# The scan's period in a hybrid decoder layer: twelve halves of weights a block in place of sixteen

## The chip, the cores and the metric

The kernel runs on one core of one Trainium2 chip. Its time is the device time of an execution in microseconds; several runs are taken and their median is given. The profile shows one execution. Five engines run their own programs and meet through semaphores: TensorE (PE, matmuls into the accumulation memory PSUM), VectorE (DVE), ScalarE (ACT), GpSimd (POOL, here only for transfers) and SyncE (SP, transfers).

## The reference

One layer of a decoder trunk on 576 tokens (512 of a prompt, 64 of eight samples with a state of their own). In essence:

```python
proj = x @ w_in                              # 2048 x 10240: u, z_a, b, c, h, z_c, g_a, g_c
# A) state space: 64 groups of 16 channels, a complex diagonal state of 64 per group
bu = einsum(u_group, bb)                     # input matrix, from lam and b
h  = associative_scan(lam, bu) + lam**t * h0
y  = Re(c @ h) + d * u
y  = gelu(y); y = y * sigmoid(y @ w_glu)
y_a = (y * silu(z_a)) @ w_out_a
# B) gated convolution of width 3
y_c = (b * conv3(c * h_c)) * silu(z_c) @ w_out_c
out = (sigmoid(g_a) * y_a + sigmoid(g_c) * y_c) @ w_o
x   = layernorm(alpha * x + out)             # also returned: the last states and convolution rows
```

All values are float32.

## The kernel before, in words

All weights stream through the core in *halves*: one half is 128 output features by 1024 input features. SyncE loads a half into one of three buffers `w_raw`. ScalarE copies it, rounded, to `w_hi` (its `split`, L764), VectorE writes the rest to `w_lo` (its `split`, L979), and TensorE multiplies: 48 matmuls of 288 columns per half for the three products hi·hi, hi·lo, lo·hi (`half`, L634). Halves are numbered h. The stretches are: u (h = 0 to 15), the convolution (16 to 79, eight halves per group of channels, l = (h − 16) mod 8), z_a (80 to 95), the gates g (96 to 159), then w_glu, w_out_c, w_out_a and w_o.

Each engine has a loop over h. In the step of h ScalarE and VectorE first split half h + 2, then do what the stretch wants (evacuate PSUM, gate, convolve), then `scan_steps(h)`. ScalarE's split of h + 2 waits until TensorE has ended half h − 1, since the buffer is used again. What reads a half's result waits for `half_done` of h + 1, which means the end of half h: in the convolution ScalarE at l = 1 and 7, VectorE at l = 3, 5 and 7; in z_a both at odd h; in the gates ScalarE at odd h.

The scan of the state space (A) runs beside this, from h = 16 on, in eight blocks of eight groups. `ssm_step(h, off)` gives the block b whose step `off` falls on half h: block b starts at S = 16 + SSM_PER·b, and its steps count halves from there. A block goes so (before, with the step in brackets):

- GpSimd loads the block's matrices (`load_mats`, −1) and u (`load_u`, 2).
- VectorE makes the table of rotations (`turn_table`, 0), the input matrix (1) and the output matrix with the small taps (2).
- ScalarE rounds the output matrix to `lch` (4), the input matrix to `lbh` and u to `uh` (5). VectorE writes the rests: `lcl` (5), `lbl` and `ul` (6).
- TensorE makes the input products (`states_in`, L656, L657) and the taps (`taps`) ahead of half S + 7. They wait for `lbl` and `ul`.
- ScalarE evacuates (7), VectorE adds (8, 9), GpSimd swaps the halves of partitions (`v_sw`, 9), VectorE runs the scan proper (`scan`, 11), GpSimd swaps again (12) and stores the taps (11) and loads them shifted, as `lth` and `ltl`, by 16 transfers (`load_lt`, 13). VectorE turns back (`turn_back`, 14); its result `st` lies in `u_raw`'s place.
- ScalarE rounds the states to `hh` (15), VectorE writes the rest `hl` (17).
- TensorE makes the outputs (`outputs`, L679 to L682) ahead of half S + 19. They wait for `hl`, `lcl` and the taps, and each engine takes its instructions in order, so the half behind waits too.
- ScalarE, VectorE: GELU (19 to 23). GpSimd stores y (`store_y`, 25).

GpSimd runs without splits. Its loop over h only sets the order of its transfers; each waits for its semaphore.

Of the kernel before, what the change touches and what calls it, by code (L numbers as in the profile page):

```python
# [60 lines left out]
SSM0 = H_CONV  # L61
SSM_PER = 16
Y_LOAD = SSM0 + SSM_PER * (BLK - 1) + 23

# [30 lines left out]
def build(nc, d):  # L95
# [79 lines left out]
    out_st = [r(f"out_st{i}", [P, TOK]) for i in range(4)]  # L175
    st = u_raw
    uh, ul = (u2[:, :, i, :] for i in range(2))
# [353 lines left out]
    def _(pool):  # L531
# [21 lines left out]
        def load_u(b):  # L553
            for s in range(2):
                pool.wait_ge(u_stored[s], 16 * (b + 2 - s) // 2 if b < NB - 1 else 16 * NB // 2)
            if b:
                pool.wait_ge(hl_ready, b)
            src = u_dram[b].rearrange("(g c) (j k) -> j c g k", c=GC, k=CH)
            for j in range(T):
                pool.dma_start(u_raw[GC * j:GC * j + GC, :, :], src[j]).then_inc(u_loaded, 16)  # L560
# [27 lines left out]
        def scan_moves(h):  # L588
            if (b := ssm_step(h, -1)) is not None:
                load_mats(b)  # L590
            if (b := ssm_step(h, 2)) is not None:
                load_u(b)
            if (b := ssm_step(h, 9)) is not None:
                pool.wait_ge(v_ready, b + 1)
                swap(v_sw, v_st, v_swapped)
            if (b := ssm_step(h, 12)) is not None:
                pool.wait_ge(s_ready, b + 1)
                swap(v_sw, v_st, s_swapped)
            if (b := ssm_step(h, 11)) is not None:
                store_k(b)  # L600
            if (b := ssm_step(h, 13)) is not None:
                load_lt(b)
            if (b := ssm_step(h, 25)) is not None:
                store_y(b)

        store_mq()
        for h in range(SSM0 - 1, SSM0 + SSM_PER * (BLK - 1) + 26):
            scan_moves(h)

    @blk.tensor  # L610
    def _(pe):
# [83 lines left out]
        for h in range(H_CONV, H_GLU):  # L695
            if (b := ssm_step(h, 7)) is not None:
                states_in(b)
                taps(b)
            if (b := ssm_step(h, 19)) is not None:
                outputs(b)  # L700
            par = (h // 2) % 2
            if h % 2 == 0:
                fresh(par)
            half(h, par, xh, xl, h % 2 * KH, h % 2 == 0, h % 2 == 1)
# [51 lines left out]
    def _(act):  # L756
# [23 lines left out]
        def scan_steps(h):  # L780
            if (b := ssm_step(h, 19)) is not None:
                act.wait_ge(y_done, b + 1)
                if b:
                    act.wait_ge(y_stored, U_LOAD * b)
                for y, o in zip(in_banks(y_pre), of_scan(0)):
                    act.activation(y, o, ACT.Copy).then_inc(y_evac, 1)
            if (b := ssm_step(h, 4)) is not None:
                act.wait_ge(lc_ready, b + 1)
                if b:
                    act.wait_ge(y_done, b)  # L790
                act.activation(lch[:, :, :, :].rearrange("p g t c -> p g (t c)"),
                               lc[:, :, 1:, :].rearrange("p g t c -> p g (t c)"), ACT.Copy).then_inc(lch_ready, 1)
            if (b := ssm_step(h, 5)) is not None:
                act.wait_ge(lb_ready, b + 1)
                act.activation(lbh[:, :, :], mb[:, :, :, :].rearrange("p g c s -> p g (c s)"), ACT.Copy)\
                   .then_inc(lbh_ready, 1)
                act.wait_ge(u_loaded, U_LOAD * (b + 1))
                act.activation(uh, u_raw[:, :, :], ACT.Copy).then_inc(uh_ready, 1)
            if (b := ssm_step(h, 7)) is not None:
                act.wait_ge(v_done, b + 1)  # L800
                if b:
                    act.wait_ge(st_ready, b)
                for v, o in zip(in_banks(v_st), of_scan(0)):
                    act.activation(v, o, ACT.Copy).then_inc(v_evac, 1)
            if (b := ssm_step(h, 7)) is not None:
                act.wait_ge(k_done, b + 1)
                if b:
                    act.wait_ge(kl_ready, b)
                act.activation(k_st[:, :, :].rearrange("p h n -> p (h n)"), k_ps[:, 0:2 * P], ACT.Copy)\
                   .then_inc(k_evac, 1)  # L810
            if (b := ssm_step(h, 10)) is not None:
                act.wait_ge(kd_ready, b + 1)
                if b:
                    act.wait_ge(k_stored, 32 * b)
                act.activation(k_hi[:, :, :], k_st[:, :, :], ACT.Copy).then_inc(kh_ready, 1)
            if (b := ssm_step(h, 15)) is not None:
                act.wait_ge(st_ready, b + 1)
                act.activation(last_state[:, b * NG:(b + 1) * NG, :], st[:, :, CP - 1:], ACT.Copy)
                act.activation(hh[:, :, 1:CP], st[:, :, 0:CP - 1], ACT.Copy)
                act.activation(hh[:, :, CP:], h0[:, 0, b * NG:(b + 1) * NG, :], ACT.Copy).then_inc(hh_ready, 1)  # L820
            if (b := ssm_step(h, 22)) is not None:
                act.wait_ge(y_arg, b + 1)
                act.activation(scr[0][:, 0:COLS], scr[0][:, 0:COLS], ACT.Sigmoid, scale=GELU_S).then_inc(y_sig, 1)
# [144 lines left out]
    def _(dve):  # L968
# [190 lines left out]
        def turn_table(b):  # L1159
            gs = slice(b * NG, (b + 1) * NG)  # L1160
            f = [fine[:, 0:T, c, gs].rearrange("p r g -> p g r").unsqueeze(2).to_broadcast([P, NG, T, T])
                 for c in (0, 1)]
            k, ks = ([t[:, 0:T, c, gs].rearrange("p a g -> p g a").unsqueeze(3).to_broadcast([P, NG, T, T])
                      for c in (0, 1)] for t in (coarse, coarse_s))
            s = [x[:, 0:NG * CP].rearrange("p (g a r) -> p g a r", g=NG, r=T) for x in scr]
            for out, a, op in ((cos, (k[0], k[1]), ALU.subtract), (sins, (ks[1], ks[0]), ALU.add)):
                own.mark(dve.tensor_tensor(s[0], a[0], f[0], ALU.mult))
                link(dve.tensor_tensor(s[1], a[1], f[1], ALU.mult))
                link(dve.tensor_tensor(grid(out), s[0], s[1], op))
# [39 lines left out]
        def scan(b):  # L1209
            s = [x[:, 0:COLS] for x in scr]  # L1210
            dve.wait_ge(v_swapped, 32 * (b + 1))
            own.mark(dve.tensor_tensor(s[0], flat(v_st), flat(cos), ALU.mult))
            link(dve.tensor_tensor(s[1], flat(v_sw), flat(sins), ALU.mult))
# [6 lines left out]
        def turn_back(b):  # L1220
            s = [x[:, 0:COLS] for x in scr]
            dve.wait_ge(s_swapped, 32 * (b + 1))
            own.mark(dve.tensor_tensor(s[0], flat(v_st), flat(cos), ALU.mult))
            link(dve.tensor_tensor(s[1], flat(v_sw), flat(sins), ALU.mult))
            dve.wait_ge(ul_ready, b + 1)
            dve.tensor_tensor(flat(st), s[0], s[1], ALU.subtract).then_inc(st_ready, 1)

        def scan_steps(h):
            if (b := ssm_step(h, 17)) is not None:
                dve.wait_ge(hh_ready, b + 1)  # L1230
                own.mark(dve.tensor_tensor(hl[:, :, 1:CP], st[:, :, 0:CP - 1], hh[:, :, 1:CP].bitcast(F32), ALU.subtract))
                dve.tensor_tensor(hl[:, :, CP:], h0[:, 0, b * NG:(b + 1) * NG, :], hh[:, :, CP:].bitcast(F32),
                                  ALU.subtract).then_inc(hl_ready, 1)
            if (b := ssm_step(h, 0)) is not None:
                turn_table(b)
            if (b := ssm_step(h, 1)) is not None:
                input_matrix(b)
            if (b := ssm_step(h, 2)) is not None:
                output_matrix(b)
            if (b := ssm_step(h, 8)) is not None:  # L1240
# [4 lines left out]
                dve.sem_inc(v_sum, 1)  # L1245
            if (b := ssm_step(h, 20)) is not None:
                dve.wait_ge(y_evac, 2 * b + 2)
# [3 lines left out]
                dve.sem_inc(y_sum, 1)  # L1251
            if (b := ssm_step(h, 5)) is not None:
                dve.wait_ge(lch_ready, b + 1)
# [4 lines left out]
            if (b := ssm_step(h, 6)) is not None:  # L1258
# [4 lines left out]
                dve.tensor_tensor(ul, u_raw[:, :, :], uh.bitcast(F32), ALU.subtract).then_inc(ul_ready, 1)  # L1263
            if (b := ssm_step(h, 9)) is not None:
                chunk_sums(b)
            if (b := ssm_step(h, 11)) is not None:
                dve.wait_ge(kh_ready, b + 1)
                dve.tensor_tensor(k_lo[:, :, :], k_st[:, :, :], k_hi[:, :, :].bitcast(F32), ALU.subtract)\
                   .then_inc(kl_ready, 1)
            if (b := ssm_step(h, 11)) is not None:  # L1270
                scan(b)
            if (b := ssm_step(h, 14)) is not None:
                turn_back(b)
            if (b := ssm_step(h, 21)) is not None:
                dve.wait_ge(y_sum, b + 1)
# [3 lines left out]
                dve.scalar_tensor_tensor(s, s, 1.0, y, ALU.add, ALU.mult).then_inc(y_arg, 1)  # L1279
            if (b := ssm_step(h, 23)) is not None:  # L1280
                dve.wait_ge(y_sig, b + 1)
# [330 lines left out]
```

## Time and profile before

| | |
|---|---|
| median of 3 runs | 1577.32 us (1576.9 to 1578.0) |
| the profiled execution | 1577.16 us, span 1575.3 us |
| TensorE busy | 1545.9 us, 98% of the span |
| VectorE busy | 830.0 us, 53% |
| ScalarE busy | 444.3 us, 28% |
| GpSimd busy | 189.0 us, 12% |
| granted clock of TensorE, mean | 0.995 of full |
| traffic of memory | 136 GB/s over the span |

A busy share is a mean over the whole span. TensorE's rows are matmuls that overlap: a matmul of 288 columns lasts some 296 ns in the profile while the next starts some 133 ns later (6.40 us for 48), so a row's end lies behind the next row's start. In a timeline the bracket at the end of a row gives the time for which the engine was idle ahead of it and what ended that.

### The profile page before, as it was taken

Reading aid. Unit: us, or ns where it says so; the run is one execution under the profiler, and the core shown is the slowest. Engines: PE = TensorE matmul, PEld = TensorE weight load, DVE = VectorE, ACT = ScalarE, POOL = GpSimd, SP = SyncE. Lnnn points to the kernel's source line nnn. Section 1 sums busy time; section 2 is a strip of 40 time slices with the busy share of each in tenths; the row PEclk is TensorE's granted clock in tenths of the full one; section 3 lists DMA queues with packets and bytes.
Section 4 is the critical chain, followed back from the end, with each engine's and each line's share of the span. In section 5 each row is a group of like instructions: output and inputs, shape, how many; then the busy total and the mean of one; then the engine's idle time right before and its main releaser. Section 6 shows DMA issues by size and latency. Waiting matters only on the chain.

```text
span 1575.3 us, 26995 instructions
## 1 busy us (share of the span) xinstructions
PE 1545.9 (98%) x11690; PEld 1539.2 (98%) x11690; DVE 830.0 (53%) x1177; ACT 444.3 (28%) x582; POOL 189.0 (12%) x348
## 2 busy tenths in 40 slices
PE   8999999999999999999999999999999999999994
PEld 8999999999999999999999999999999999999994
DVE  5977374464463553643633533223733355666887
ACT  4222222222122122222222222133411122333444
POOL 0110040230311311302204113010000000000000
PEclk9999999999999999999999999999999999999997
DMA  9352362452543543634625535344544443555573
GB/s 304 125 152 91 92 166 79 116 158 75 133 133 94 146 117 122 176 109 132 161 83 165 136 115 147 104 156 150 189 141 134 125 127 125 160 187 183 183 221 107
DMA packets 87447, 221.21 MB, mean 140 GB/s; under 512 B 19744, under 2 KB 28576, under 8 KB 87328
## 3 DMA queue, kind: packets, MB, share of 16 engines
q1 hardware_dynamic: 71456, 188.78, 38.6%
q0 software_dynamic: 15872, 30.70, 8.6%
q8 instruction: 92, 1.51, 0.4%
q14 instruction: 27, 0.22, 0.0%
HBM read 186.55 MB, written 28.16 MB: 136 GB/s over the span
## 4 chain that ended last, share of the span: by engine, by line
PE 94%; DVE 3%; SPq 1%; DMA 1%; issue 1%; ACT 0%; DVEq 0%
PE acc L634 91%; SPq L420 1%; DMA w_raw<-in_w 1%; PE s_ps L656 1%; DVE r_all L1495 0%; PE s_ps L680 0%; PE s_ps L682 0%; DVE w_lo L979 0%; DVE r_all L1494 0%; PE s_ps L657 0%; PE s_ps L681 0%; PE s_ps L679 0%; PE k_ps L666 0%; DVE rstd L1488 0%; DVE r_all L1460 0%
## 5 line engine op out<-in xcount | busy, mean ns | idle before, releaser
L634 PE MATMUL acc<-xh,w_hi 128*128 128x288 f32 x2560 | 550.9, 297 | 3.9 <-DVE xl L987 3.7
L634 PE MATMUL acc<-xh,w_lo 128*128 128x288 f32 x2560 | 549.5, 296 | 0.0
L634 PE MATMUL acc<-xl,w_hi 128*128 128x288 f32 x2560 | 549.2, 296 | 0.0
L979 DVE TENSOR_TENSOR w_lo<-w_raw,w_hi 128x1024 fp32r<-128x1024 f32 x263 | 321.8, 1224 | 406.8 <-ACT w_hi L764 405.1
L764 ACT ACTIVATE w_hi<-w_raw 128x1024 fp32r<-128x1024 f32 x263 | 278.0, 1058 | 597.3 <-PE acc L634 578.2
L634 PEld LDWEIGHTS acc<-xh,w_hi 128*128 128x128 f32 x2560 | 412.9, 189 | 6.4 <-DVE w_lo L997 2.3
L634 PEld LDWEIGHTS acc<-xh,w_lo 128*128 128x128 f32 x2560 | 413.4, 188 | 0.0
L634 PEld LDWEIGHTS acc<-xl,w_hi 128*128 128x128 f32 x2560 | 413.4, 188 | 0.0
L634 PE MATMUL acc<-mh,w_hi 128*128 128x288 f32 x512 | 152.2, 297 | 1.0 <-DVEq L983 0.7
L634 PE MATMUL acc<-ml,w_hi 128*128 128x288 f32 x512 | 151.3, 296 | 0.0
L634 PE MATMUL acc<-mh,w_lo 128*128 128x288 f32 x512 | 151.3, 296 | 0.0
L634 PEld LDWEIGHTS acc<-mh,w_hi 128*128 128x128 f32 x512 | 96.1, 188 | 1.7 <-DVEq L983 0.9
L634 PEld LDWEIGHTS acc<-ml,w_hi 128*128 128x128 f32 x512 | 96.1, 188 | 0.2
L634 PEld LDWEIGHTS acc<-mh,w_lo 128*128 128x128 f32 x512 | 96.1, 188 | 0.0
L887 ACT ACTIVATE out_st<-acc 128x576 f32<-128x576 f32 x32 | 20.9, 654 | 189.6 <-PE acc L634 189.6
L564 POOL DMA_DIRECT2D v_sw<-v_st x32 | 18.3, 577 | 446.4 <-DVE v_st L1204 417.7
L634 PE MATMUL acc<-gcl,w_hi 128*128 128x288 f32 x256 | 55.0, 296 | 0.0
L634 PE MATMUL acc<-gch,w_lo 128*128 128x288 f32 x256 | 55.0, 296 | 0.0
L634 PE MATMUL acc<-gal,w_hi 128*128 128x288 f32 x256 | 55.0, 296 | 0.0
L634 PE MATMUL acc<-gah,w_hi 128*128 128x288 f32 x256 | 55.0, 296 | 0.0
L634 PE MATMUL acc<-gah,w_lo 128*128 128x288 f32 x256 | 54.9, 296 | 0.0
L634 PE MATMUL acc<-gch,w_hi 128*128 128x288 f32 x256 | 54.9, 296 | 0.0
(275 smaller groups left out, 1467.1 us busy)
## 6 DMA issues: line engine op xcount, KB each, us to landing
w_raw<-in_w SPq DMA_DIRECT2D x263, 512.0 KB, 3.8
sg_dram<-out_st SPq DMA_DIRECT2D x32, 288.0 KB, 4.6
v_sw<-v_st POOLq DMA_DIRECT2D x32, 144.0 KB, 3.9
gc_in<-sg_dram SPq DMA_DIRECT2D x16, 288.0 KB, 2.7
sz_in<-sg_dram SPq DMA_DIRECT2D x16, 288.0 KB, 2.7
x_in<-in_xT SPq DMA_DIRECT2D x32, 144.0 KB, 2.2
outT<-o_st SPq DMA_DIRECT2D x32, 144.0 KB, 1.8
mb<-mq_dram POOLq DMA_DIRECT2D x8, 512.0 KB, 6.6
```

Of the source, the lines that this page charges most:

```text
L420: sp.dma_start(k_dram[part, b, :, :, 0:KROW - T * GC].rearrange("x p n -> p x n"), zeros[:, :, :]).then_inc(zeros_stored, 16)
L564: pool.dma_start(to[64 * x:64 * x + 64, :, :], of[64 - 64 * x:128 - 64 * x, :, :]).then_inc(done, 16)
L634: ins = pe.matmul(acc[:, par, t, 0:TH], w, m[:, k0 + k, t * TH:(t + 1) * TH], start=first and k == 0 and n == 0, stop=last and k == KH - 1 ...
L656: pe.matmul(out_of(g), lbh[:, g, :], u, start=True, stop=False)
L764: act.activation(w_hi[h % NW][:, :], w_raw[:, h % NW, :], ACT.Copy).then_inc(hi_ready, 1)
L887: act.activation(two(out_st[n % 4][:, :]), halves_of(acc[:, n % 2]), ACT.Sigmoid).then_inc(g_sig, 1)
L979: dve.tensor_tensor(w_lo[h % NW][:, :], w_raw[:, h % NW, :], w_hi[h % NW][:, :].bitcast(F32), ALU.subtract).then_inc(lo_ready, 1)
```

## The change

`SSM_PER` goes from 16 to 12: block b starts at half 16 + 12b. The steps are set anew, with the input products still at 7 and the outputs at 16 in place of 19.

```diff
-SSM_PER = 16
-Y_LOAD = SSM0 + SSM_PER * (BLK - 1) + 23
+SSM_PER = 12
+Y_LOAD = H_GLU - NB - 1
...
-    st = u_raw
+    st = v_sw
...
             if b:
-                pool.wait_ge(hl_ready, b)
+                pool.wait_ge(ul_ready, b)
...
         def scan_moves(h):
-            if (b := ssm_step(h, -1)) is not None:
+            if (b := ssm_step(h, 0)) is not None:
                 load_mats(b)
...
-            if (b := ssm_step(h, 12)) is not None:
+            if (b := ssm_step(h, 21)) is not None:
+                store_y(b)
+            if (b := ssm_step(h, 10)) is not None:
+                store_k(b)
+            if (b := ssm_step(h, 11)) is not None:
                 pool.wait_ge(s_ready, b + 1)
                 swap(v_sw, v_st, s_swapped)
-            if (b := ssm_step(h, 11)) is not None:
-                store_k(b)
-            if (b := ssm_step(h, 13)) is not None:
                 load_lt(b)
-            if (b := ssm_step(h, 25)) is not None:
-                store_y(b)
...
-            if (b := ssm_step(h, 19)) is not None:
+            if (b := ssm_step(h, 16)) is not None:
                 outputs(b)
...
-            if (b := ssm_step(h, 4)) is not None:
+            if (b := ssm_step(h, 5)) is not None:
                 act.wait_ge(lc_ready, b + 1)
...
+            if (b := ssm_step(h, 6)) is not None:
                 act.wait_ge(u_loaded, U_LOAD * (b + 1))
...
+            if b:
+                dve.wait_ge(st_ready, b)
...
+            if b:
+                dve.wait_ge(y_made, b)
...
-            dve.wait_ge(ul_ready, b + 1)
+            dve.wait_ge(dve_step, own.value())
             dve.tensor_tensor(flat(st), s[0], s[1], ALU.subtract).then_inc(st_ready, 1)
...
-            if (b := ssm_step(h, 17)) is not None:
+            if (b := ssm_step(h, 15)) is not None:
                 dve.wait_ge(hh_ready, b + 1)
...
```

The other steps go like this (before, after): `turn_table` 0, 2; `input_matrix` 1, 3; `output_matrix` 2, 4; `lcl` 5, 6; `chunk_sums` 9, 8; `k_hi` 10, 9; `scan` and `k_lo` 11, 10; `turn_back` 14, 13; `hh` 15, 14; y: 19, 20, 21, 22, 23 to 16, 17, 18, 19, 20. Unmoved are `lbh` (5), `lbl` and `ul` (6), the evacuation (7), the sum (8) and the first swap (9). GpSimd's `store_y` of a block now stands behind the first swap of the next, as before, and its `store_k` ahead of the second swap.

Every engine's work for a half stays in place, and the scan's rows move against it. On VectorE, around `hl` of block 0 (L1231 and L1232 before; L1235 and L1236 now), before:

```order
L1379 TENSOR_TENSOR gate_t<-gate_t,acc 128x576
L1381 TENSOR_TENSOR conv_t_90<-conv_t_90,gate_t 128x576
L979 TENSOR_TENSOR w_lo<-w_raw,w_hi 128x1024
L1167 TENSOR_TENSOR scr_77<-coarse,fine 128x512
L1168 TENSOR_TENSOR scr_78<-coarse,fine 128x512
L1169 TENSOR_TENSOR cos<-scr_77,scr_78 128x8x64
L1167 TENSOR_TENSOR scr_77<-coarse_s,fine 128x512
L1168 TENSOR_TENSOR scr_78<-coarse_s,fine 128x512
L1169 TENSOR_TENSOR sins<-scr_77,scr_78 128x8x64
L979 TENSOR_TENSOR w_lo<-w_raw,w_hi 128x1024
L1231 TENSOR_TENSOR h_84<-u_raw,h_84 128x8x63
L1232 TENSOR_TENSOR h_84<-h_51,h_84 128x8x8
```

And in the changed kernel (the last two rows are the next block's `input_matrix`):

```order
L979 TENSOR_TENSOR w_lo<-w_raw,w_hi 128x1024
L1383 TENSOR_TENSOR gate_t<-gate_t,acc 128x576
L1385 TENSOR_TENSOR conv_t_90<-conv_t_90,gate_t 128x576
L1235 TENSOR_TENSOR h_84<-v_sw,h_84 128x8x63
L1236 TENSOR_TENSOR h_84<-h_51,h_84 128x8x8
L1177 TENSOR_TENSOR scr_77<-mb,bc 128x1024
L1178 TENSOR_TENSOR scr_78<-mb,bc 128x8x64
```

`hl` stood behind the next block's rotations and a split, two halves after the gate's operations of l = 7 (L1379, L1381). Now it stands directly behind these operations (L1383, L1385), which wait for the end of their half, and the rotations are ahead of them.

On ScalarE, around `lch`, `lbh` and `uh` (here `u_69`) of block 1, before:

```order
L764 ACTIVATE w_hi<-w_raw 128x1024
L791 ACTIVATE lch<-lc 128x1024
L764 ACTIVATE w_hi<-w_raw 128x1024
L859 ACTIVATE last_conv<-q_pad 128x18
L795 ACTIVATE lbh<-mb 128x1024
L798 ACTIVATE u_69<-u_raw 128x8x72
L764 ACTIVATE w_hi<-w_raw 128x1024
```

And in the changed kernel (`gate_t` L853 is the evacuation at l = 1, which waits for the end of its half):

```order
L763 ACTIVATE w_hi<-w_raw 128x1024
L853 ACTIVATE gate_t<-acc 128x576
L790 ACTIVATE lch<-lc 128x1024
L794 ACTIVATE lbh<-mb 128x1024
L763 ACTIVATE w_hi<-w_raw 128x1024
L798 ACTIVATE u_69<-u_raw 128x8x72
L763 ACTIVATE w_hi<-w_raw 128x1024
```

`lch` stood a step ahead of `lbh`. Now both stand behind the evacuation of l = 1 and ahead of the next split, and `uh` stands behind that split.

## Rows read from the trace of the kernel before

**Rows 1.** The page's first part: busy time of each engine.
```profile
PE 1545.9 (98%) x11690; PEld 1539.2 (98%) x11690; DVE 830.0 (53%) x1177; ACT 444.3 (28%) x582; POOL 189.0 (12%) x348
```

**Rows 2.** Waits of TensorE: line, waited for, total us, times, longest.
```profile
PE s_ps L656 <- issue: 1.3, 6, 0.3
```

**Rows 3.** Timeline, block 4 in z_a: start us, duration us, engine, line, operation.
```profile
587.38 0.65 ACT L872 ACTIVATE out_st<-acc 128x576 f32<-128x576 f32 x1 [5.28 <-PE acc L634]
...
587.93 1.05 ACT L795 ACTIVATE lbh<-mb 128x1024 fp32r<-128x1024 f32 x1
...
588.88 0.68 ACT L798 ACTIVATE u<-u_raw 128x576 fp32r<-128x576 f32 x1
...
589.05 1.23 DVE L1254 TENSOR_TENSOR lcl<-lc,lch 128x1024 fp32r<-128x1024 f32 x1
...
592.79 1.22 DVE L1260 TENSOR_TENSOR lbl<-mb,lbh 128x1024 fp32r<-128x1024 f32 x1
...
593.92 0.75 DVE L1263 TENSOR_TENSOR u<-u_raw,u 128x576 fp32r<-128x576 f32 x1
...
594.78 0.30 PE L656 MATMUL s_ps<-u,lbh 128*128 128x144 f32 x1 [1.03 <-DVE lbl L1260]
```

**Rows 4.** Timeline of ScalarE: two splits, one half apart.
```profile
152.03 1.06 ACT L764 ACTIVATE w_hi<-w_raw 128x1024 fp32r<-128x1024 f32 x1 [3.71 <-PE acc L634]
158.43 1.06 ACT L764 ACTIVATE w_hi<-w_raw 128x1024 fp32r<-128x1024 f32 x1 [5.34 <-PE acc L634]
```

**Rows 5.** Timeline around the end of half 31 (l = 7).
```profile
218.28 0.43 PE L634 MATMUL acc<-xh,w_hi 128*128 128x288 f32 x2
...
218.49 0.65 ACT L862 ACTIVATE gate_t<-acc 128x576 f32<-128x576 f32 x1 [5.28 <-PE acc L634]
...
220.93 1.23 DVE L979 TENSOR_TENSOR w_lo<-w_raw,w_hi 128x1024 fp32r<-128x1024 f32 x1
```

**Rows 6.** Timeline of VectorE: hl of block 0, input_matrix, a split, output_matrix.
```profile
229.15 0.68 DVE L1231 TENSOR_TENSOR h<-u_raw,h 128x504 fp32r<-128x504 f32 x1
229.74 0.22 DVE L1232 TENSOR_TENSOR h<-h,h 128x64 fp32r<-128x64 f32 x1
229.88 1.22 DVE L1175 TENSOR_TENSOR scr<-mb,bc 128x1024 f32<-128x1024 f32 x1
...
239.46 1.22 DVE L979 TENSOR_TENSOR w_lo<-w_raw,w_hi 128x1024 fp32r<-128x1024 f32 x1
```

**Rows 7.** Timeline of VectorE behind the end of half 19 (l = 3).
```profile
139.27 0.17 DVE L1360 COPY q_pad<-conv_par 128x16 f32<-128x16 f32 x1 [3.54 <-PE acc L634]
...
140.60 1.22 DVE L979 TENSOR_TENSOR w_lo<-w_raw,w_hi 128x1024 fp32r<-128x1024 f32 x1
...
142.29 1.67 DVE L1370 SCALAR_TENSOR_TENSOR conv_t<-q_pad,conv_par,conv_t 128x576 f32<-128x576 f32 x2
```

**Rows 8.** Timeline of ScalarE behind the end of half 17 (l = 1).
```profile
126.37 0.65 ACT L853 ACTIVATE gate_t<-acc 128x576 f32<-128x576 f32 x1 [5.28 <-PE acc L634]
127.20 1.06 ACT L764 ACTIVATE w_hi<-w_raw 128x1024 fp32r<-128x1024 f32 x1 [0.17 <-ACT gate_t L853]
```

**Rows 9.** Timeline of VectorE and GpSimd: half 27's end, the swap, last tap loads.
```profile
192.99 0.17 DVE L1360 COPY q_pad<-conv_par 128x16 f32<-128x16 f32 x1 [4.12 <-PE acc L634]
...
199.36 1.36 POOL L564 DMA_DIRECT2D v_sw<-v_st  x2 [3.57 <-DVE v_st L1218]
...
216.45 1.05 POOL L580 DMA_DIRECT2D ltl<-k_dram  x2 [2.37 <-issue]
```

**Rows 10.** The second tap tile (ltl): us from issue to landing.
```profile
DMA to landing us min/median/max: 2.5/2.7/5.6
```

**Rows 11.** Waits of GpSimd: issue gaps at the first tap tile (lth).
```profile
POOL lth L580 <- issue: 43.0, 13, 5.5
```

**Rows 12.** Windows at the span's end: busy us of each engine, granted clock.
```profile
1556.00:1558.00 2.00, 0.00 (x0) 0.00 (x0) 1.96 (x1) 0.00 (x0) 0.00 (x0) 1.00 0.00 0
1558.00:1560.00 2.00, 0.00 (x0) 0.00 (x0) 1.89 (x5) 0.51 (x1) 0.00 (x0) 0.55 0.00 0
```

More of the change, by code:

```diff
@@ L595, in scan_moves @@
                 swap(v_sw, v_st, v_swapped)
-            if (b := ssm_step(h, 12)) is not None:
+            if (b := ssm_step(h, 21)) is not None:
[3 more added lines that the diff above has]
+            if (b := ssm_step(h, 11)) is not None:
                 pool.wait_ge(s_ready, b + 1)
                 swap(v_sw, v_st, s_swapped)
-            if (b := ssm_step(h, 11)) is not None:
-                store_k(b)
-            if (b := ssm_step(h, 13)) is not None:
                 load_lt(b)
-            if (b := ssm_step(h, 25)) is not None:
-                store_y(b)
         store_mq()
-        for h in range(SSM0 - 1, SSM0 + SSM_PER * (BLK - 1) + 26):
+        for h in range(SSM0, SSM0 + SSM_PER * (BLK - 1) + 26):
             scan_moves(h)
@@ L780, in scan_steps @@
         def scan_steps(h):
-            if (b := ssm_step(h, 19)) is not None:
+            if (b := ssm_step(h, 16)) is not None:
                 act.wait_ge(y_done, b + 1)
@@ L810, in scan_steps @@
                    .then_inc(k_evac, 1)
-            if (b := ssm_step(h, 10)) is not None:
+            if (b := ssm_step(h, 9)) is not None:
                 act.wait_ge(kd_ready, b + 1)
@@ L815, in scan_steps @@
                 act.activation(k_hi[:, :, :], k_st[:, :, :], ACT.Copy).then_inc(kh_ready, 1)
-            if (b := ssm_step(h, 15)) is not None:
+            if (b := ssm_step(h, 14)) is not None:
                 act.wait_ge(st_ready, b + 1)
@@ L820, in scan_steps @@
                 act.activation(hh[:, :, CP:], h0[:, 0, b * NG:(b + 1) * NG, :], ACT.Copy).then_inc(hh_ready, 1)
-            if (b := ssm_step(h, 22)) is not None:
+            if (b := ssm_step(h, 19)) is not None:
                 act.wait_ge(y_arg, b + 1)
@@ L1233, in scan_steps @@
                                   ALU.subtract).then_inc(hl_ready, 1)
-            if (b := ssm_step(h, 0)) is not None:
+            if (b := ssm_step(h, 2)) is not None:
                 turn_table(b)
-            if (b := ssm_step(h, 1)) is not None:
+            if (b := ssm_step(h, 3)) is not None:
                 input_matrix(b)
-            if (b := ssm_step(h, 2)) is not None:
+            if (b := ssm_step(h, 4)) is not None:
                 output_matrix(b)
@@ L1245, in scan_steps @@
                 dve.sem_inc(v_sum, 1)
-            if (b := ssm_step(h, 20)) is not None:
+            if (b := ssm_step(h, 17)) is not None:
                 dve.wait_ge(y_evac, 2 * b + 2)
@@ L1251, in scan_steps @@
                 dve.sem_inc(y_sum, 1)
-            if (b := ssm_step(h, 5)) is not None:
+            if (b := ssm_step(h, 6)) is not None:
                 dve.wait_ge(lch_ready, b + 1)
@@ L1263, in scan_steps @@
                 dve.tensor_tensor(ul, u_raw[:, :, :], uh.bitcast(F32), ALU.subtract).then_inc(ul_ready, 1)
-            if (b := ssm_step(h, 9)) is not None:
+            if (b := ssm_step(h, 8)) is not None:
                 chunk_sums(b)
-            if (b := ssm_step(h, 11)) is not None:
+            if (b := ssm_step(h, 10)) is not None:
                 dve.wait_ge(kh_ready, b + 1)
@@ L1269, in scan_steps @@
                    .then_inc(kl_ready, 1)
-            if (b := ssm_step(h, 11)) is not None:
+            if (b := ssm_step(h, 10)) is not None:
                 scan(b)
-            if (b := ssm_step(h, 14)) is not None:
+            if (b := ssm_step(h, 13)) is not None:
                 turn_back(b)
-            if (b := ssm_step(h, 21)) is not None:
+            if (b := ssm_step(h, 18)) is not None:
                 dve.wait_ge(y_sum, b + 1)
@@ L1279, in scan_steps @@
                 dve.scalar_tensor_tensor(s, s, 1.0, y, ALU.add, ALU.mult).then_inc(y_arg, 1)
-            if (b := ssm_step(h, 23)) is not None:
+            if (b := ssm_step(h, 20)) is not None:
                 dve.wait_ge(y_sig, b + 1)
```

## The prediction

> **What bounds the kernel now.** I read the page's first part: TensorE is busy for 98% of the span [rows 1]. Next come TensorE's own waits: the eight blocks of the scan cost it 1.3 us of short issue gaps [rows 2] and one wait of 1.0 us for VectorE [rows 3]. So the span is a queue of matmuls, and nothing that another engine does earlier can win more than these 2.3 us. The change leaves every matmul as it is. The question is only whether TensorE, which takes its rows in order, meets a wait that isn't over.
>
> Then I looked, engine by engine, at what happens around the end of a half of weights. A half takes 6.40 us: ScalarE starts the split of the half after next each time TensorE ends one, at 152.03 and at 158.43 [rows 4]. ScalarE and VectorE therefore walk through the program in step with TensorE. Their operations of a step h come when half h starts, but behind any wait for the end of half h which stands ahead of them in that step. In the convolution's eight halves (l = 0 to 7) ScalarE waits so at l = 1 and 7, VectorE at l = 3, 5 and 7; in the z_a and gate stretches that follow, ScalarE at each odd half, and VectorE too in z_a's. With sixteen halves a block, each offset of the scan always met the same l. With twelve, l alternates between two values. I call a block's start S; it is 16 + 12b.
>
> **First term: the products of the outputs wait for hl.** VectorE makes hl at S+15 (it was S+17) and TensorE wants it at the start of S+16 (it was S+19). S+15 is l = 7 for blocks 0, 2 and 4, l = 3 for blocks 1 and 3, an odd half of z_a for block 5. In all six VectorE first waits for the end of half S+15, which is when TensorE is at the products. So the wait is the time from that end until hl is there, and half S+16 queues behind it.
> - At l = 7: ScalarE wakes at 218.49; VectorE, behind two multiplications, is free at 220.93 [rows 5]. hl takes 0.81 us from the start of its first operation to the end of its second [rows 6]. TensorE starts 0.11 us after VectorE's last write (594.67 to 594.78) [rows 3]. That makes 221.85, where the next matmul started at 218.28 [rows 5]: 3.57 us. Three blocks: 10.7 us.
> - At l = 3: VectorE wakes at 139.27 and is free at 140.60 [rows 7]: 1.33 + 0.81 + 0.11 = 2.25 us, and 0.21 for the time between TensorE's start and an engine's waking, as in the case above: 2.46 us. Two blocks: 4.9 us.
> - In z_a: ScalarE wakes at 587.38, VectorE is free at 589.05 [rows 3]: 1.67 + 0.81 + 0.11 + 0.21 = 2.8 us. One block.
> - Blocks 6 and 7 have S+15 in the gate stretch, where VectorE waits for no half: nothing.
> Sum: 18.4 us. In the trace of before hl stands two halves ahead and the products show no wait at all.
>
> **Second term: the input products wait for lbl and ul.** These want ul at the start of S+7. lch moves from step 4 to 5 beside lbh, uh from 5 to 6, lcl on VectorE from 5 to 6. For blocks 1 and 3 step S+5 is l = 1, so ScalarE does lch and lbh only after the end of S+5. From that end: evacuation and its own wait 0.83 us [rows 8]; lch, lbh, then the split of S+8, each 0.95 after the other (587.93 to 588.88) [rows 3]; the split takes 1.06 [rows 4] and ends at 3.79. VectorE takes it up some 0.1 later, then split, lcl, lbl and ul 1.13 apart and ul for 0.75 [rows 3]: 8.03, with TensorE's 0.11 8.14. The half lasts 6.40, and ScalarE wakes a few hundredths behind its end: an idle of 1.8 us. Block 7 (S+5 an odd gate half) I take alike. In z_a, blocks 5 and 6, ScalarE is through 0.28 us earlier (lbh starts 0.55 after it wakes [rows 3]): 1.5 us. Block 0 has another cause: input_matrix and output_matrix now follow the convolution's operations at l = 3 and 4. From the end of S+3: 1.33, then 9.58 for the two with a split between them [rows 6], and 2.2 for the convolution (3.36 from 140.60 with a split of 1.13 in it [rows 7]), 13.1 against two halves of 12.8; with the waking and the last operation's own end lch starts some 0.5 into S+6, and it ends like z_a's: 1.6 us. Sum: 3 × 1.8 + 2 × 1.5 + 1.6 = 10.0 us. Blocks 2 and 4 (l = 5 and 6) have ScalarE free; VectorE's split, lcl, lbl and ul come behind its multiplication and y_sum and end about 6.0 us into S+6: no wait, by 0.4 us. Of the 2.3 us of before, 1.9 stand within these six waits: net 8.1 us.
>
> **What costs nothing.** GpSimd's own program: the swap of the states follows store_k, load_lt at once. Before, that swap started at 199.36, 6.37 us after VectorE woke from half S+11 (192.99), a whole half; its last tap load was issued by 217.50 [rows 9] and lands up to 5.6 us later [rows 10]: 23.7 us, 3.7 halves. With the scan one step earlier and the same distance it starts by S+12 and is through at S+15.7, before S+16, and hl is later still. load_u waits for ul instead of hl, which frees it earlier. The extra waits on VectorE (st_ready, y_made, its own step) are for operations of its own queue that lie halves back. Y_LOAD is 151 by the old rule and by the new. What VectorE does per block is now in 12 halves, but it is busy for 53% [rows 1]. Bounds on all this: from 0 to the 6.4 us that one block would lose if its tap loads came a half later.
>
> Sum: 18.4 + 8.1 = 26.5 us on the profiled execution's 1577.2: 1603.7 us. That execution lies 0.2 below the median, no matter here. For either term the lower bound is its absence (1585.3, 1595.6); the upper one is that each of the twelve waits costs 0.6 us more, a further VectorE operation of the size of ul or hl ahead of it, and blocks 2 and 4 lose 0.5 each: 1612.
>
> **Rivals.**
> - *The waits stay hidden (not slower).* If hl and ul came ahead of the products as before, all that is left is that block 4's late lbl goes: 1577.2 − 1.0 = 1576.2, no change. For it: products at S+19 never waited. Against: it needs hl's operations ahead of VectorE's wait for the end of half S+15, and in the new order they stand behind it. It decides from the point where hl starts less than 6.4 − 0.9 us into S+15. 4%.
> - *GpSimd becomes late.* It spent 43.0 us in issue gaps at the first half of the tap loads [rows 11], 5.4 us a block. Doubled, the taps land 5.4 − 1.9 = 3.5 us after S+16's start: no later than hl at l = 7, 1.0 later at l = 3, 0.7 in z_a, and 3.5 in blocks 6 and 7, which had no wait: 9.7 us, 1613. For it: in each period as many transfers stand in twelve halves as in sixteen. Against: GpSimd is busy 12% [rows 1]. The Trainium skill (SBUF — State Buffer, section "SBUF: two separate sides") has a rule for it: a VectorE operation in a two-port mode keeps GpSimd from writing descriptors. By it the convolution's short copies would stretch these issues; the trace has the gaps but doesn't name their cause. 5%.
> - *TensorE's clock falls in the new waits.* The longest is 3.4 us of idle. At the end of the span TensorE is idle from 1556 to 1558, and the granted clock was full there (2.4 GHz); it fell to half (1.2 GHz) in 1558 to 1560 [rows 12]. So the level outlasted a pause of 2 us and more. If it fell in each of the three waits at l = 7 and came back within the products and one half, it would cost up to 3.5 + 6.4 us each: 1633. The Trainium skill (TensorE: Matmul & The Clock Gate, section "HAM oscillation — how this bites in real kernels") says that pauses of TensorE between bursts throttle the clock again; by that rule this would be the time. 5%.
> - *Only one term comes true:* 1585 or 1596, where ScalarE or VectorE runs further ahead than I take it to. 6%.
>
> **How the numbers follow.** Forecast 1604 us, 80%; its own range is 1598 to 1610. The range for 8 in 10 reaches down to the case of the first term alone and up to the bound on sizes: 1595 to 1612. A measurement here tells about 0.2% (3.2 us) from no change. Faster by that would need more than all of TensorE's waits in the scan: 1%, and I leave 2%. Within it: the first rival, 4%. Slower: the rest, 94%.
>
> **What would show it.** TensorE's waits in the new profile: the first products of the outputs (s_ps from lth) wait on VectorE's h six times, 2.3 to 3.6 us each, none in blocks 6 and 7; the first input products (s_ps from lbh) wait on VectorE's u about six times, 1.5 to 1.9 us. TensorE's busy time stays near 1546 us and the span grows by about 26 us, all of it before block 7's outputs (half 116); the granted clock stays at full level. It would be wrong if the products' wait ends on a DMA (taps), if blocks 6 and 7 wait as long as the others, or if the span grows behind half 116.

## The result, and the profile after

The kernel with the change takes 1635.77 us (median of 4 runs, 1634.32 to 1636.74) where the one before takes 1577.36 beside it (4 runs, 1576.9 to 1578.0): a ratio of 1.0369, with a 95% interval of 1.0351 to 1.0387. It is slower, as forecast, but by 58.4 us and not by 26.5; the time lies above the range of 1595 to 1612.

I look first at the page of the kernel after: the line of the engines, answering [rows 1], and TensorE's granted clock in 40 slices of the span (1633.3 us; it was 1575.3).

```profile
PE 1579.4 (97%) x11690; PEld 1570.8 (96%) x11690; DVE 830.9 (51%) x1177; ACT 444.6 (27%) x582; POOL 187.3 (11%) x348
```

```profile
PEclk9999989999898999899999999999999999999997
```

The span grew by 58.0 us. TensorE executes the same 11690 matmuls, but is busy for 1579.4 us with them where it was for 1545.9: 33.5 us of the loss are matmuls that last longer. The other 24.5 us are idle time (53.9 us of the span; it was 29.4). The slices with an 8 stand between the sixth and the twentieth, the part of the program in which the scan runs.

The idle time is where the forecast put it. TensorE's waits in the kernel after (engine, line, waited for: us in total, times, longest), answering [rows 2]:

```profile
PE s_ps L678 <- DVE h L1236: 17.0, 6, 3.2
PE s_ps L655 <- DVE lbl L1264: 8.3, 5, 2.0
...
PE s_ps L655 <- DVE u L1267: 1.7, 1, 1.7
```

Six waits at the outputs' products (L678), six at the input products (L655): 27.0 us. Block by block the first are 3.23, 2.42, 3.23, 2.34, 3.23 and 2.56 us in blocks 0 to 5, none in 6 and 7; the second are 1.65, 1.71, 1.71, 1.43, 1.43 and 1.99 us in blocks 0, 1, 3, 5, 6 and 7, none in 2 and 4.

The timeline of the kernel after behind the end of half 31 (start us, duration us, engine, line, operation, idle before), answering [rows 5, 6]:

```profile
219.81 0.65 ACT L862 ACTIVATE gate_t<-acc 128x576 f32<-128x576 f32 x1 [5.28 <-PE acc L633]
...
220.57 0.75 DVE L1383 TENSOR_TENSOR gate_t<-gate_t,acc 128x576 f32<-128x576 f32 x1 [2.18 <-ACT gate_t L862]
221.47 0.76 DVE L1385 TENSOR_TENSOR conv_t<-conv_t,gate_t 128x576 f32<-128x576 f32 x1
222.14 0.68 DVE L1235 TENSOR_TENSOR h<-v_sw,h 128x504 fp32r<-128x504 f32 x1
222.74 0.22 DVE L1236 TENSOR_TENSOR h<-h,h 128x64 fp32r<-128x64 f32 x1
...
223.01 0.33 PE L678 MATMUL s_ps<-u,lth 128*128 128x144 f32 x1 [3.23 <-DVE h L1236]
```

This is the chain of the first term: VectorE wakes behind ScalarE's evacuation of the ended half, does two multiplications, then hl, and TensorE starts 0.05 us after its last row ends. Matmuls normally start 0.13 us apart; this one starts 3.53 us after the one ahead, so it is 3.40 late where 3.57 were forecast.

The timeline of block 1 at l = 1, ScalarE, VectorE and TensorE, answering [rows 3, 8]:

```profile
244.43 0.65 ACT L853 ACTIVATE gate_t<-acc 128x576 f32<-128x576 f32 x1 [5.28 <-PE acc L633]
245.25 1.06 ACT L790 ACTIVATE lch<-lc 128x1024 fp32r<-128x1024 f32 x1 [0.17 <-ACT gate_t L853]
246.22 1.04 ACT L794 ACTIVATE lbh<-mb 128x1024 fp32r<-128x1024 f32 x1
247.17 1.04 ACT L763 ACTIVATE w_hi<-w_raw 128x1024 fp32r<-128x1024 f32 x1
...
248.24 1.23 DVE L979 TENSOR_TENSOR w_lo<-w_raw,w_hi 128x1024 fp32r<-128x1024 f32 x1 [7.10 <-ACT w_hi L763]
...
249.38 1.22 DVE L1258 TENSOR_TENSOR lcl<-lc,lch 128x1024 fp32r<-128x1024 f32 x1
...
250.52 1.22 DVE L1264 TENSOR_TENSOR lbl<-mb,lbh 128x1024 fp32r<-128x1024 f32 x1
...
251.65 0.75 DVE L1267 TENSOR_TENSOR u<-u_raw,u 128x576 fp32r<-128x576 f32 x1
...
252.50 0.31 PE L655 MATMUL s_ps<-u,lbh 128*128 128x144 f32 x1 [1.71 <-DVE lbl L1264]
```

This is the second term: one row of operations with hardly a gap, 8.07 us from ScalarE's waking to TensorE's start, in a half of 6.40. The wait's releaser is given as lbl, though ul ends last: TensorE waits for both, one after the other (`lbl_ready`, `ul_ready`).

What the forecast did not have shows in the windows of the scan and of the stretches behind these two waits (stretch, its length, busy us of TensorE, its weight load, VectorE, ScalarE and GpSimd with counts, granted clock, DMA share, GB/s):

```profile
150.00:820.00 670.00, 643.06 (x4701) 637.13 (x4700) 357.48 (x454) 155.57 (x221) 159.49 (x293) 0.95 0.45 120
...
200.00:223.57 23.57, 20.34 (x154) 20.11 (x153) 15.06 (x18) 5.81 (x9) 9.28 (x18) 1.00 0.65 158
223.57:233.81 10.24, 10.24 (x47) 10.24 (x47) 8.83 (x12) 0.71 (x2) 0.12 (x1) 0.50 0.33 85
233.81:250.00 16.19, 16.19 (x123) 16.19 (x123) 3.71 (x5) 5.24 (x6) 0.00 (x0) 1.00 0.10 33
...
254.29:257.70 3.41, 3.41 (x27) 2.87 (x27) 0.71 (x1) 1.67 (x4) 0.00 (x0) 0.50 0.43 144
```

Over the scan the mean clock is 0.95. 0.56 us after TensorE has resumed at 223.01, the clock falls to half (1.2 GHz) and stays there for 10.24 us, in which it starts 47 matmuls (27 of them the outputs' short ones of 144 columns); in the next 16.19 us, at full clock (2.4 GHz), it starts 123. Ten such stretches stand in this trace, each behind one of the twelve waits (not at the input products of blocks 0 and 5), of 3.41, 6.83 or 10.24 us, 71.7 us in all; from 803.83 us on the clock is full until TensorE has ended its work.

### The profile page after: what moved, and what is told of

Same layout as the page of the kernel before. It is cut to its first block, busy times and chain, and to the rows that moved or that the text cites. A ratio compares the mean times of both kernels' runs of the same rounds, so it can differ in the third digit from the quotient of the medians.

```text
span 1633.3 us, 26999 instructions
## 1 busy us (share of the span) xinstructions
PE 1579.4 (97%) x11690; PEld 1570.8 (96%) x11690; DVE 830.9 (51%) x1177; ACT 444.6 (27%) x582; POOL 187.3 (11%) x348
## 4 chain that ended last, share of the span: by engine, by line
PE 92%; DVE 5%; ACT 1%; issue 1%; DMA 1%; SPq 0%; DVEq 0%; ACTq 0%
PE acc L633 87%; PE s_ps L678 1%; PE s_ps L681 1%; PE s_ps L680 1%; PE s_ps L679 1%; DVE w_lo L979 1%; PE s_ps L655 1%; DMA x_raw<-in_xT 1%; PE s_ps L656 0%; DVE r_all L1499 0%; DVE lcl L1258 0%; DVE r_all L1498 0%; DVE lbl L1264 0%; ACT w_hi L763 0%; PE k_ps L665 0%
## 5 line engine op out<-in xcount | busy, mean ns | idle before, releaser
L633 PE MATMUL acc<-xh,w_hi 128*128 128x288 f32 x2560 | 557.8, 300 | 3.8 <-DVE xl L987 3.8
L633 PE MATMUL acc<-xl,w_hi 128*128 128x288 f32 x2560 | 555.2, 299 | 0.0
L633 PEld LDWEIGHTS acc<-xh,w_hi 128*128 128x128 f32 x2560 | 419.9, 192 | 6.6 <-issue 2.3
L633 PEld LDWEIGHTS acc<-xl,w_hi 128*128 128x128 f32 x2560 | 419.7, 191 | 0.0
L633 PEld LDWEIGHTS acc<-xh,w_lo 128*128 128x128 f32 x2560 | 419.0, 191 | 0.0
```

Of the source, the lines that this page charges most:

```text
L633: ins = pe.matmul(acc[:, par, t, 0:TH], w, m[:, k0 + k, t * TH:(t + 1) * TH], start=first and k == 0 and n == 0, stop=last and k == KH - 1 ...
```

## The experiments

Three kernels part the time first. The step of hl can stand earlier (e1), the low halves of the matrices later (e2), or both (e3). If the waits are all there is, e3 must give back everything.

**e1: the outputs' waits taken away.** VectorE makes hl right behind the split of its step, ahead of the multiplications that wait for the half (in the loops of the convolution, z_a and gate stretches).

```diff
-        def scan_steps(h):
+        def low_states(h):
             if (b := ssm_step(h, 15)) is not None:
...
+        def scan_steps(h):
...
             split(h + 2)
+            low_states(h)
```

> hl is made ahead of VectorE's wait for the end of half S+15, so the six waits of the outputs' products (17.0 us) should go; the input products' waits stay. Theory A (each pause of TensorE lets its clock fall, and the clock costs some 32 us, 23 of them behind the outputs' pauses by their share of the time at half clock): about 1594 us, half clock only behind the input products' pauses. Rival B (the clock falls for another reason that comes with the shorter period, such as more small matmuls or transfers per time): only the 18 us of the waits go, 1617 us.

Measured: 1595.02 us (4 runs, 1587.9 to 1597.46), ratio 1.0100 [1.0071, 1.0129]. TensorE's waits in this kernel, and its window of the scan:

```profile
PE s_ps L655 <- DVE lbl L1266: 8.3, 5, 2.0
...
PE s_ps L655 <- DVE u L1269: 1.6, 1, 1.6
```

```profile
150.00:820.00 670.00, 659.98 (x4991) 654.96 (x4990) 372.60 (x472) 165.22 (x234) 172.04 (x316) 0.98 0.48 128
```

No wait at the outputs is left, those at the inputs are unchanged, and the clock still falls behind five of the six, which are 1.4 to 2.0 us long: 27.3 us at half clock. I had taken only the long waits for able to do that. The wide spread of the four runs fits a number and length of falls that differ from one execution to the next (e8): their mean granted clocks go with their times, 0.986, 0.985, 0.989 and 0.993 for 1597.46, 1597.34, 1592.71 and 1587.9 us.

**e2: the input products' waits taken away.** The split of C (lch, lcl) stands behind uh on ScalarE and behind ul on VectorE; only the outputs need it.

```diff
             if (b := ssm_step(h, 5)) is not None:
-                act.wait_ge(lc_ready, b + 1)
-                if b:
-                    act.wait_ge(y_done, b)
-                act.activation(lch...).then_inc(lch_ready, 1)
...
             if (b := ssm_step(h, 6)) is not None:
...
+                act.wait_ge(lc_ready, b + 1)
+                if b:
+                    act.wait_ge(y_done, b)
+                act.activation(lch...).then_inc(lch_ready, 1)
```

> lch and lcl go behind uh and ul, so the input products' waits (10.0 us in six blocks) should go; the outputs' waits stay. Theory A: 1619 us (1577 + 18 of waits + 23 of clock), no half clock behind half S+7. Rival B: 1627 us.

Measured: 1613.04 us (4 runs, 1611.1 to 1613.99), ratio 1.0220 [1.0205, 1.0235]. Its waits and window:

```profile
PE s_ps L678 <- DVE h L1235: 16.9, 6, 3.2
```

```profile
150.00:820.00 670.00, 653.07 (x4868) 649.43 (x4867) 366.68 (x464) 159.21 (x226) 169.49 (x312) 0.96 0.47 125
```

The six waits at the outputs stay, and behind all six the clock falls: 47.8 us at half clock. Theory A's picture holds; its time was 6 us too high, since without waits the kernel is faster than the one before (e3), and the six stretches are shorter in all than behind the same waits in the changed kernel (51.2 us).

**e3: both.**

> Both of the two edits: no wait of either kind with the period of twelve halves. Theory A: the clock stays full and the time is that of the kernel before or up to 2 us under it, 1575 to 1577 us. Rival B (the period itself brings the clock down): 1609 us.

Measured: 1573.81 us (9 runs, 1573.44 to 1574.71), ratio 0.9974 [0.9964, 0.9984]. TensorE's waits (the first of them; none at s_ps in the scan) and its window:

```profile
PE acc L633 <- DVE xl L986: 2.9, 2, 1.5
PE k_ps L687 <- DVE zeros L989: 1.2, 1, 1.2
```

```profile
150.00:820.00 670.00, 669.91 (x5173) 667.45 (x5172) 378.06 (x479) 169.11 (x240) 172.60 (x316) 1.00 0.49 131
```

TensorE is busy for all of the scan, at full clock. So the changed order has no cost beyond these twelve waits, GpSimd's part included, and rival B, that the period itself brings the clock down, falls. This version is a little faster than both kernels: 4.0 us under the one before beside it (12 runs, 1577.77; 3.3 between the spans of the two traces). The short waits of the one before [rows 2, 3] cost 2.3 us of idle and, with seven starts each 0.17 us later than a matmul that overlaps the one ahead, 3.5.

From here the sum is to be read against 1573.8: after loses 62.0 us to it, 29.0 in the waits (27.0 of idle and 12 × 0.17) and the remaining 33.0 in the clock. (The two were timed apart; the kernel before took 1577.77 beside the one and 1577.36 beside the other, and these 0.4 us are not taken out.)

**e4: the waits kept, the clock kept.** Ahead of each wait TensorE gets unused matmuls of 256 columns, whose result nothing reads, as many as fill the idle time: by block, the first list at the input products, the second at the outputs.

```diff
+        def fill(n):
+            for _ in range(n):
+                pe.matmul(k_ps[:, 256:512], xh[:, 0, 0:P], xh[:, 0, 0:256], start=True, stop=True)
...
+                fill((15, 15, 0, 15, 0, 13, 13, 18)[b])
...
+                fill((28, 21, 28, 20, 28, 22, 0, 0)[b])
```

> The changed kernel with matmuls that are used by nothing (256 columns, into free columns of the taps' bank) ahead of each of the twelve waits, as many as fill it: TensorE arrives at the same waits but is busy meanwhile. Theory A: the waits' time stays and the clock doesn't fall: 1604 us, clock 0.995. Rival B: the clock falls as in the changed kernel: 1635 us. If the fill is too long, each block loses some tenths more than in A.

Measured: 1603.21 us (4 runs, 1603.12 to 1603.87), ratio 1.0160 [1.0145, 1.0175]. The timeline of TensorE and VectorE at the end of half 31, and the window:

```profile
220.62 3.52 PE L649 MATMUL k_ps<-xh 128*128 128x256 f32 x28
...
223.75 0.22 DVE L1242 TENSOR_TENSOR h<-h,h 128x64 fp32r<-128x64 f32 x1
...
224.02 0.33 PE L682 MATMUL s_ps<-u,lth 128*128 128x144 f32 x1
```

```profile
150.00:820.00 670.00, 670.00 (x5181) 666.90 (x5181) 370.75 (x469) 164.04 (x233) 172.59 (x316) 1.00 0.47 127
```

The products start as late as in the changed kernel, right behind hl. TensorE does 28 useless matmuls in the meantime, and the clock never falls. The same lateness then costs 25.4 us over the kernel before (1577.77 beside it), where 26.5 were forecast: the forecast's sum is the time of the changed kernel without the clock. The 32.6 us between this run and the changed kernel are the clock's.

**e5, e6, e7: how long a pause does it?** On e3, which has no pause, eleven pauses are put ahead of plain halves of the gate stretch. TensorE waits there for 1, 2 or 4 VectorE operations whose result isn't used: 1, 2, 4 in turn (e5), always 1 (e6), always 4 (e7).

```diff
+    PAUSES = {120: 1, 123: 2, 126: 4, 129: 1, 132: 2, 135: 4, 138: 1, 141: 2, 144: 4, 147: 1, 150: 2}
...
+            if h in PAUSES:
+                pe.wait_ge(paused, sorted(PAUSES).index(h) + 1)
...
+                for _ in range(PAUSES[h + 1]):
+                    link(dve.tensor_tensor(conv_t[0][:, :], conv_t[1][:, :], conv_t[1][:, :], ALU.max))
+                dve.sem_inc(paused, 1)
```

> The version without waits (both edits of before), with eleven pauses of TensorE put between plain halves of the gate stretch (every third half from 120), far from the scan: VectorE lets each half go after one, two or four operations of 0.79 us that follow the end of the half ahead, so some 1.0, 1.8 or 3.3 us of idle in turn (4, 4 and 3 times), 23 us in all with the overlap of the matmuls. Theory A (a pause alone brings the clock down): half clock behind most of the pauses of two and four operations, none or few behind those of one; at 3.3 us a fall 1620 us. Rival B (it takes the scan's small matmuls beside the pause): no fall, 1597 us.

> The same with one operation at each of the eleven pauses, some 1.0 us of idle each, 13 us in all. Theory A by the one pause of 1.03 us of the kernel before, which kept the clock: no fall, 1587 us. Rival C (any pause can do it): falls behind some, up to 1620 us.

> The same with four operations at each pause, some 3.3 us of idle each, 38 us in all. Theory A: a fall behind every one, 3.3 us each or more: about 1648 us. Rival B: no fall, 1612 us.

Measured: e5 1605.42 us (1607.38, 1603.47), ratio 1.0178 [1.0149, 1.0208]; e6 1588.89 (1588.63, 1589.15), 1.0073 [1.0044, 1.0103]; e7 1632.26 (1631.97, 1632.56), 1.0348 [1.0318, 1.0378]. TensorE's wait at the pauses and the window that holds them, of e5, then e6, then e7:

```profile
PE acc L635 <- DVEq L1417: 21.4, 11, 3.4
```

```profile
820.00:1090.00 270.00, 248.62 (x1778) 246.04 (x1777) 67.50 (x67) 53.77 (x60) 4.20 (x8) 0.96 0.34 100
```

```profile
PE acc L635 <- DVEq L1417: 11.1, 11, 1.0
```

```profile
820.00:1090.00 270.00, 258.93 (x1923) 256.35 (x1922) 63.49 (x61) 60.00 (x68) 4.20 (x8) 1.00 0.37 110
```

```profile
PE acc L635 <- DVEq L1417: 37.2, 11, 3.4
```

```profile
820.00:1090.00 270.00, 232.76 (x1585) 230.18 (x1584) 74.46 (x78) 45.91 (x50) 4.19 (x8) 0.92 0.29 87
```

Pauses of 1.0 us leave the clock full in all 15 cases (4 in e5, 11 in e6). Pauses of 1.8 us bring it down in 3 of 4, pauses of 3.4 us in 14 of 14. The first of e7 in windows, pause, fall and return:

```profile
827.00:832.57 5.57, 2.19 (x16) 1.95 (x15) 4.58 (x6) 2.28 (x3) 0.00 (x0) 1.00 0.01 3
832.57:835.98 3.41, 3.41 (x17) 3.41 (x16) 0.35 (x1) 0.00 (x0) 2.76 (x6) 0.50 0.69 206
835.98:851.00 15.02, 15.02 (x114) 15.02 (x114) 2.45 (x2) 2.77 (x3) 1.43 (x3) 1.00 0.31 79
```

Ahead of plain halves the clock comes back after 3.41 us nearly always. So a fall is cheap there: e7 lies 58.5 us above e3, the pauses' own lateness is 11 × 3.55 = 39.1, and 19.4 are left, 1.8 us for each of eleven falls; the traced execution of e5 (1607.38) gives 1.7 (33.6 − 23.2, by six). Theory A had 3.3, from the changed kernel. What differs is the length of the stretches, not their price: e7 loses 19.4 of 44.4 us at half clock, the changed kernel 33.0 of 71.7. Rival B in e5 and e7, that it takes the scan's small matmuls beside the pause, falls with these falls ahead of plain halves; rival C in e6, that any pause can do it, finds none at 1.0 us. e6 came out 2.2 us above 1586.7, which is e3 and 11 × 1.17; its trace has one half-clock stretch of 6.83 us, at none of the eleven pauses but behind a wait of 1.87 us for VectorE at the start of the program.

**e8: the changed kernel once more, unaltered.** Are the same waits hit each time?

> The changed kernel once more, unchanged, for a second trace. Theory A (the pauses are the program's, the fall's time is not): the twelve waits have the same lengths to 0.1 us, the falls stand behind other ones of them and last otherwise, some 60 to 80 us at half clock in all. Rival D (each wait has its own fixed fall): the same ten falls of the same lengths.

Measured: 1633.68 us (one run). The waits are the same to 0.1 us, the falls are not. The windows around block 0's input products, of the kernel after and then of this run:

```profile
157.60:159.30 1.70, 0.18 (x2) 0.00 (x0) 1.70 (x3) 1.06 (x1) 0.00 (x0) 1.00 0.75 272
...
161.00:165.00 4.00, 4.00 (x43) 3.72 (x43) 0.00 (x0) 0.00 (x0) 0.00 (x0) 1.00 0.40 131
```

```profile
157.60:159.30 1.70, 0.28 (x3) 0.04 (x1) 1.70 (x2) 1.06 (x1) 0.00 (x0) 1.00 0.77 275
...
161.00:165.00 4.00, 4.00 (x32) 3.46 (x32) 0.00 (x0) 0.00 (x0) 0.00 (x0) 0.57 0.42 131
```

The same pause of 1.65 us costs nothing beyond its length in one execution and a stretch of 3.41 us at half clock besides in the other. In this run all six input waits are hit and five of six output waits (not block 3's): 68.3 us at half clock in eleven stretches. Rival D, that a wait's place decides, falls: which wait is hit, and for how long, changes from run to run.

**e9: the pauses shortened, not filled.** As e4 with 8 matmuls fewer ahead of each wait, so that 0.78 to 0.90 us of idle are left.

```diff
-                fill((15, 15, 0, 15, 0, 13, 13, 18)[b])
+                fill((7, 7, 0, 7, 0, 5, 5, 10)[b])
...
-                fill((28, 21, 28, 20, 28, 22, 0, 0)[b])
+                fill((20, 13, 20, 12, 20, 14, 0, 0)[b])
```

> The changed kernel with the same unused matmuls ahead of the twelve waits, but some eight fewer at each, so that about 1.0 us of each wait is left as idle time ahead of the scan's small matmuls. Theory A' (a pause of 1.0 us doesn't bring the clock down, here as little as between plain halves): no fall, 1603 us as with the whole fill. Rival E (ahead of the scan's small matmuls a shorter pause is enough): falls behind several, 1608 us and up.

Measured: 1605.23 us (1605.94, 1604.52), ratio 1.0176 [1.0147, 1.0206]. TensorE's waits:

```profile
PE s_ps L682 <- DVE h L1242: 5.1, 6, 0.9
PE s_ps L659 <- DVE lbl L1270: 4.2, 5, 0.9
```

Twelve pauses under 1 us, and one fall (6.83 us, behind block 3's outputs). With e3, where the same products follow no pause and no fall comes, this says that it is the pause that brings the clock down, not the products behind it. Even under 1 us it isn't quite safe here, while at plain halves 1.0 us never did it.

## Why the prediction was wrong

**The first term was right.** The forecast had six waits for hl in blocks 0 to 5 and none in 6 and 7, and that is what stands in the trace. Late starts against forecast: 3.40 and 3.57 (l = 7), 2.58 and 2.50 against 2.46 (l = 3), 2.73 and 2.8 (z_a); the sum 18.0 against 18.4.

**The second term was right.** Blocks 0, 1, 3, 5, 6 and 7 wait, 2 and 4 do not. Idle against forecast: 1.71, 1.71 and 1.99 against 1.8 each, 1.43 twice against 1.5, 1.65 against 1.6; the sum 9.9 against 10.0. What was taken off for the kernel before was read wrongly, without harm to the result: of its 2.3 us, 1.0 stands in these six blocks and 1.3 in blocks 2 and 4, and all of it goes, so that 2.3 and not 1.9 come off. e4, with both terms and no fall, is 25.4 us above the kernel before; forecast 26.5.

**What was costed at nothing was nothing.** GpSimd's transfers did not become late: no wait in the scan ends on a DMA, and e3 shows no wait there at all. The rival on GpSimd's issue gaps falls with it.

**The step that failed is the rival on the clock: "So the level outlasted a pause of 2 us and more", from [rows 12], and with it the 5%.** There, TensorE stands idle while the clock is full, and I read that as the clock bearing a pause. So the sum carried nothing for the clock; the runs put it at 32.6 us (e4 against the changed kernel). Of the signs named ahead the waits came as said, but TensorE's busy time is 1579.4 us and not some 1546, and its clock 0.95 over the scan and not full. The same stretch of the kernel before in windows of 1 us shows what it was:

```profile
1554.00:1555.00 1.00, 0.47 (x2) 0.01 (x1) 0.50 (x2) 0.41 (x1) 0.00 (x0) 1.00 0.00 0
...
1557.00:1558.00 1.00, 0.00 (x0) 0.00 (x0) 0.97 (x1) 0.00 (x0) 0.00 (x0) 1.00 0.00 0
1558.00:1559.00 1.00, 0.00 (x0) 0.00 (x0) 0.93 (x3) 0.00 (x0) 0.00 (x0) 0.61 0.00 0
```

The last matmul ends at 1554.5, and the clock falls some 3.7 us later (0.61 as a mean of that window puts it near 1558.2). In the changed kernel, the ten falls come 1.9 to 4.9 us after TensorE went idle, nine of them when it was already at work again: the wait of half 31 began at 219.78, ended at 223.01, and the clock fell at 223.57. The fall follows the pause with a delay. [Rows 12] can't tell a pause that is borne from one whose answer is still on its way, because nothing followed there; I took a delay for a tolerance.

The size failed with it. I had allowed at most three falls, at the long waits of l = 7. Over the changed kernel, its second run, e1 and e2 the clock fell at 17 of 18 waits for outputs (2.3 to 3.2 us) and at 15 of 18 for inputs (1.4 to 2.0). A stretch at half clock costs nearly half its length: 33.0 of 71.7 us in the changed kernel, 3.3 us a fall. The rival's own price, up to 9.9 us a fall, was three times too high and its count less than a third of the ten. Its total of 1633 came near the measured time only because the two errors cancel: that is luck.

The Trainium skill (TensorE: Matmul & The Clock Gate, section "HAM oscillation — how this bites in real kernels") describes a kernel in which TensorE waits between bursts of matmuls and begins each burst at the low clock. The runs agree that such waits bring the clock down (32 of 36 in the scan). They differ in that waits of 1.4 to 3.2 us are enough here, where the page's are some 3 to 5 us, and in that the fall mostly comes when TensorE is at work again. I had cited the section, and set [rows 12] above it.

What stays open: behind the outputs' waits the clock stays low for 6.8 or 10.2 us, at plain halves for 3.4 nearly always. The length of the pause doesn't explain it, since pauses of 3.4 us at plain halves have the short stretch. TensorE resumes there with the outputs' products (L678 to L681) and not with a half; whether that matters, no run tests. By themselves these products don't bring the clock down, as e3 shows.

Open too is why the start of the program is different. There TensorE waits for VectorE (`xl`) in every trace, 17 times for 1.5 to 2.2 us while the clock is full, and the clock fell behind one of them (e6). The longest, in the kernel before, and the work behind it:

```profile
8.17:10.31 2.14, 0.00 (x0) 0.03 (x1) 1.77 (x3) 1.62 (x3) 0.00 (x0) 1.00 1.04 407
10.31:12.15 1.84, 1.83 (x12) 1.60 (x12) 0.53 (x1) 0.00 (x0) 0.00 (x0) 1.00 1.04 410
```

In the scan, pauses as long as these brought the clock down in 15 of 18 cases. So the length of a pause alone doesn't decide.

## What to carry to other kernels

Where a long queue of matmuls is full, as in the scan and the gates here, a new wait of 1.4 us or more mostly costs twice: its own length, and here on the mean 3.3 us a fall for the slow matmuls behind it (1.7 to 1.8 ahead of plain halves); add that to the sum for every such wait, not for the longest alone. When two loops of different period share engines, write down for each block beside which step of the other loop it now falls: here two groups of operations made up the loss (hl stood behind a wait, lch and lcl ahead of what TensorE needed first), and moving both (e3) turned 3.7% slower into 0.3% faster without giving up the new period. Moving hl alone (e1) left it 1.0% slower. If such a wait can't be taken away, useless matmuls in it win back what the clock would cost (1635.8 to 1603.2 us in e4).

## What the runs showed of the hardware

- The clock answers short pauses: 0 of 15 at 1.0 us, 3 of 4 at 1.8 us and 14 of 14 at 3.4 us ahead of plain halves; 1 of 12 at 0.8 to 0.9 us ahead of the scan's products.
- In the scan, 17 of 18 waits of 2.3 to 3.2 us and 15 of 18 of 1.4 to 2.0 us brought the clock down; at the start of the program 1 of 17 of 1.5 to 2.2 us did.
- The fall comes late, 1.9 to 5.0 us after the wait began over all traces, most often when TensorE is at work again (41 of 49 in the changed kernel, e8, e1, e2, e5 and e7); so it is seen in the rows behind a wait, not in it.
- Whether a pause of 1.4 to 2.3 us brings the clock down, and how long it stays down, differs between executions of one kernel (e8). e1's four runs spread over 9.6 us, e3's nine, with no fall in the traced one, over 1.3 us.
